# The third block's recurrent branch: order of its column chunks and gate products, packing of the gates' weights, and a few operations on other engines

## The reference, cut to what matters

```python
proj = h @ w_in                                  # 1024 x 2048
u, gate = split(proj)                            # 1024 columns each
uc = conv_b + sum_j up[:, j:j + T] * conv_w[j]   # causal, width 4
ub = uc.reshape(B, T, 4, 256)                    # four groups
r = sigmoid(einsum('btgi,gij->btgj', ub, w_rg) + b_rg)
i = sigmoid(einsum('btgi,gij->btgj', ub, w_ig) + b_ig)
log_a = -8 * r * softplus(-lam)
a = exp(log_a)
mult = sqrt(-expm1(2 * log_a));  mult[t = 0] = 1
h_t = a_t * h_(t-1) + mult_t * i_t * uc_t        # over all 272 rows
y = (h * silu(gate)) @ w_out
```

## Time and profile before

| | us |
|---|---|
| median of three runs | 2482.13 |
| lowest and highest of them | 2480.46, 2484.95 |
| the profiled execution | 2470.93 |
| its span, first to last instruction | 2469.5 |
| recurrent mixer to the end of the span, from PE's first column instruction at 2341.9 | 127.6 |
| PE, DVE, ACT, POOL busy in that stretch | 92.2, 85.2, 60.5, 0.0 |

### The profile page before, as it was taken

How to read it: one execution, slowest core, us unless ns; L and a number is a source line. 1 busy time by engine, 2 the same in 40 slices (tenths; PEclk the granted TensorE clock), 3 DMA queues, 4 the chain that set the end, 5 groups by cost and what they waited for, 6 DMA issues and landing times.

```text
span 2469.5 us, 29520 instructions
## 1 busy us (share of the span) xinstructions
PE 2040.5 (83%) x12478; PEld 1372.8 (56%) x12478; DVE 988.3 (40%) x1689; ACT 731.2 (30%) x1160; POOL 22.5 (1%) x27
## 2 busy tenths in 40 slices
PE   5998867777787777776778799889889899889895
PEld 3555412333333333342334499769888898766694
DVE  2542412211222221223434344577654545553475
ACT  4322221110111110113111243544444544434444
POOL 0000000000000000000000000000000000000000
PEclk7988889899999999888889899999999999899797
DMA  8948799999999999999999855434245455420430
GB/s 351 359 152 311 266 406 413 409 409 411 413 412 409 409 409 410 404 403 411 398 408 410 325 181 180 160 97 142 94 145 164 143 187 169 134 98 19 135 111 17
DMA packets 228243, 672.09 MB, mean 272 GB/s; under 512 B 11520, under 2 KB 134528, under 8 KB 187792
## 3 DMA queue, kind: packets, MB, share of 16 engines
q1 hardware_dynamic: 228112, 670.21, 71.5%
HBM read 669.12 MB, written 1.05 MB: 271 GB/s over the span
## 4 chain that ended last, share of the span: by engine, by line
PE 54%; DMA 30%; DVE 11%; ACT 4%; issue 1%; SPq 0%; POOL 0%; DVEq 0%; ACTq 0%
DMA ring<-in_w 21%; PE pb L227 12%; PE pb L228 11%; PE pb L229 11%; DMA ring<-in_w_a 5%; PE pb L1635 3%; DVE WB L310 3%; DMA ring<-in_w_in 3%; PE pb L677 2%; PE pb L1658 2%; DMA ring<-in_w_mod 1%; ACT WB L304 1%; PE pb L1619 1%; PE pb L840 1%; PE pb L868 1%
## 5 line engine op out<-in xcount | busy, mean ns | idle before, releaser
L310 DVE TENSOR_TENSOR WB<-ring,WB 128x1024 fp32r<-128x1024 f32 (+3 forms) x370 | 425.3, 1191 | 495.2 <-ACT WB L304 494.9
L304 ACT ACTIVATE WB<-ring 128x1024 fp32r<-128x1024 f32 (+3 forms) x370 | 361.3, 1025 | 774.4 <-DMA ring<-in_w_a 466.2
L227 PE MATMUL pb<-HH,WB 128*128 128x256 f32 (+1 forms) x1680 | 496.9, 296 | 15.5 <-DVE HL L3133 4.7
L228 PE MATMUL pb<-HL,WB 128*128 128x256 f32 (+1 forms) x1680 | 486.3, 289 | 0.0
L229 PE MATMUL pb<-HH,WB 128*128 128x256 f32 (+1 forms) x1680 | 485.6, 289 | 0.0
L1635 PE MATMUL pb<-ring,big 128*32 128x512 f32 x2048 | 296.5, 671 | 151.5 <-DMA ring<-in_w 134.1
L227 PEld LDWEIGHTS pb<-HH,WB 128*128 128x128 f32 x1680 | 332.2, 198 | 41.4 <-issue 21.6
L228 PEld LDWEIGHTS pb<-HL,WB 128*128 128x128 f32 x1680 | 332.2, 198 | 2.5 <-issue 2.4
L229 PEld LDWEIGHTS pb<-HH,WB 128*128 128x128 f32 x1680 | 331.6, 197 | 0.0
L1635 PEld LDWEIGHTS pb<-ring,big 128*32 128x32 f32 x2048 | 46.8, 113 | 366.1 <-DMA ring<-in_w 279.6
L1658 PE MATMUL pb<-ring,big 128*32 128x512 f32 x1024 | 168.3, 644 | 61.9 <-DMA ring<-in_w 53.9
(11 more groups left out here) (416 smaller groups left out, 1989.3 us busy)
## 6 DMA issues: line engine op xcount, KB each, us to landing
ring<-in_w SPq DMA_DIRECT2D x384, 1024.0 KB, 14.5
ring<-in_w_a SPq DMA_DIRECT2D x66, 1024.0 KB, 12.1
ring<-in_w_in SPq DMA_DIRECT2D x38, 1024.0 KB, 6.8
ring<-in_w_b SPq DMA_DIRECT2D x33, 1024.0 KB, 5.1
ring<-in_w_ada SPq DMA_DIRECT2D x32, 1024.0 KB, 6.8
ring<-in_w_mod SPq DMA_DIRECT2D x24, 1024.0 KB, 8.8
ring<-in_w_out SPq DMA_DIRECT2D x8, 1024.0 KB, 5.3
ring<-in_b_w_in SPq DMA_DIRECT2D x8, 1024.0 KB, 6.6
```

What stands on the lines that cost most here:

```text
L227: pe.matmul(o, l[0], r[0], start=start, stop=False)
L228: pe.matmul(o, l[0], r[1], start=False, stop=False)
L304: act.activation(WB[:, c % 2, 0, x:y], flat[:, x:y], ACT.Copy).then_inc(*A(("high", c, z)))
L310: dve.tensor_tensor(WB[:, c % 2, 1, x:y], flat[:, x:y], WB[:, c % 2, 0, x:y].bitcast(F32), ALU.subtract).then_inc(*V(("low", c, z), *([("f ...
```

## The change

- The chunks are put in another order: u's four chunks (s_3+12 to 15), a chunk with both gates' weights for groups 0 and 1 (16), the gate branch's first (17), both gates' weights for groups 2 and 3 (18), the gate branch's other three (19 to 21). A gate chunk is loaded by two DMAs of 512 KB.
- PE's order follows: u's columns, gate products of groups 0 and 1, columns of the gate branch, groups 2 and 3, three more column chunks. u's blocks use banks 0 to 3, all gate products banks 4 to 7, so that group g waits for the sigmoids of g-1.
- u's halves no longer lie over the input. They take the columns 272 to 407 of `HH` and `HL`, each block of 272 as two pieces of 136.
- The copy out of PSUM into `pad3` goes from DVE to ACT, with four buffers in place of two.
- The high and low halves, sigmoids, tanh and logarithms are done group by group among the chunks. Three groups of silu come after the square roots.
- POOL makes i*u, and a squared in place of ACT's exp(2 log_a).
- DVE's states and gating are separate steps: states(0), gated(0), gated(1), split of chunk 22, states(1) before the first operand; then one states(g) after each of two splits.

```diff
-           + [x for p in range(4) for x in (cols256(I["b_w_in_3"][0], 256 * p), cols256(I["b_w_in_3"][0], D + 256 * p))]
-           + [(I[n][0].rearrange("g (a p) n -> p g a n", p=128), 2048, "p (g a n) -> p g a n", dict(g=4, a=2))
-              for n in ("b_w_rg_3", "b_w_ig_3")] + rows2(I["b_w_out_3"][0]))
+           + [cols256(I["b_w_in_3"][0], 256 * p) for p in range(4)]
+           + [lru_gates(0), cols256(I["b_w_in_3"][0], D), lru_gates(2)]
+           + [cols256(I["b_w_in_3"][0], D + 256 * p) for p in range(1, 4)] + rows2(I["b_w_out_3"][0]))
...
+    def u_half(t, o):
+        return t[:, 2 * (o % 4):2 * (o % 4) + 2, T3:T3 + T3 // 2]
+    def u_halves(t, g):
+        return t[:, 4 * (g % 2):4 * (g % 2) + 4, T3:T3 + T3 // 2]
...
+        def recurrence_gates(c, g):
+            hi, lo = chunk(c)
             pe.wait_ge(*at("u_halves", g))
             for f in range(2):
                 for q in range(2):
+                    if f == 0:
+                        pe.wait_ge(*at("low", c, q))
+                    if g:
+                        pe.wait_ge(*at("ri", g - 1, f, q))
                     for kk in range(2):
+                        e = mm3(pe, PB[4 + 2 * f + q][:, 0:T3].rearrange("p (s t) -> p s t", s=2),
+                                (hi[:, q, g % 2, kk, 128 * f:128 * f + 128], lo[:, q, g % 2, kk, 128 * f:128 * f + 128]),
+                                (u_half(HH, 2 * g + kk), u_half(HL, 2 * g + kk)), kk == 0, kk == 1)
...
+        for p in range(4):
+            columns(s_3 + 12 + p, 2 * (p % 2), ("u_in", p),
+                    [("u_out", p - 2, f) if p >= 2 else ("turned", "b3", 4 + 2 * p + f, 0) for f in range(2)])
+        for g in range(2):
+            recurrence_gates(s_3 + 16, g)
+        columns(s_3 + 17, 0, ("g_in", 0), [("u_out", 2, f) for f in range(2)])
+        for g in range(2, 4):
+            recurrence_gates(s_3 + 18, g)
+        columns(s_3 + 19, 2, ("g_in", 1), [("u_out", 3, f) for f in range(2)])
+        columns(s_3 + 20, 0, ("g_in", 2), [("g_out", 0, f) for f in range(2)])
+        columns(s_3 + 21, 4, ("g_in", 3), [("ri", 3, 0, f) for f in range(2)])
...  ACT
+        sp_.upto(s_3 + 13)
+        pads(0)
+        sp_.upto(s_3 + 14)
+        pads(1)
+        high(0)
+        sp_.upto(s_3 + 15)
+        pads(2)
+        high(1)
+        sp_.upto(s_3 + 16)
+        pads(3)
+        sp_.upto(s_3 + 17)
+        sigmoids(0)
+        high(2)
+        sigmoids(1)
+        tanh(0)
+        high(3)
+        sp_.upto(s_3 + 18)
+        tanh(1)
+        silu(0)
+        sp_.upto(s_3 + 19)
+        sigmoids(2)
+        sigmoids(3)
+        tanh(2)
+        sp_.upto(s_3 + 20)
+        tanh(3)
         act.wait_ge(*last("a"))
         for g, p in enumerate(PAIRS):
             act.activation(al[:, p, :], al[:, p, :], ACT.Exp).then_inc(*A(("a", g)))
-        sp_.upto(s_3 + 22)
+        sp_.upto(s_3 + 21)
         for g, p in enumerate(PAIRS):
             act.wait_ge(*at("expm1", g))
             act.activation(ml[:, p, :], uT[:, p, :], ACT.Sqrt, scale=-1.0).then_inc(*A(("mult", g)))
+        sp_.upto(s_3 + 22)
+        for p in range(1, 4):
+            silu(p)
...  DVE
+        sp_.upto(s_3 + 13)
+        conv(0)
+        sp_.upto(s_3 + 14)
+        conv(1)
+        low(0)
+        sp_.upto(s_3 + 15)
+        conv(2)
+        low(1)
+        sp_.upto(s_3 + 16)
+        conv(3)
+        sp_.upto(s_3 + 17)
+        logs(0)
+        low(2)
+        logs(1)
+        low(3)
+        sp_.upto(s_3 + 19)
+        logs(2)
+        logs(3)
+        sp_.upto(s_3 + 20)
+        for g in range(4):
+            expm1(g)
+        sp_.upto(s_3 + 21)
+        states(0)
+        gated(0)
+        gated(1)
         sp_.upto(s_3 + 22)
+        states(1)
         dve_operand(dve, "wob", 0, gT3[:, 0, :], T3)
         for n in range(8):
             if n < 7:
-                recur(n + 1)
+                if n:
+                    gated(n + 1)
                 dve_operand(dve, "wob", n + 1, gT3[:, n + 1, :], T3)
             if n % 2 == 0:
                 sp_.upto(s_3 + 23 + n // 2)
+                if n < 4:
+                    states(n // 2 + 2)
...  POOL
+        for g, p in enumerate(PAIRS):
+            pool.wait_ge(*at("ri", g, 1, 1))
+            pool.tensor_tensor(bl3[:, p, :], bl3[:, p, :], uT[:, p, :], ALU.mult).then_inc(*G(("iu", g)))
+        for g, p in enumerate(PAIRS):
+            pool.wait_ge(*at("a", g))
+            pool.wait_ge(*last("g"))
+            pool.tensor_tensor(uT[:, p, :], al[:, p, :], al[:, p, :], ALU.mult).then_inc(*G(("a_squared", g)))
```

More of the change, by code:

```diff
@@ L281, in _build @@
            + rows2(I["a_w_out_3"][0])
[L282 to L284 removed]
+           + [cols256(I["b_w_in_3"][0], 256 * p) for p in range(4)]
+           + [lru_gates(0), cols256(I["b_w_in_3"][0], D), lru_gates(2)]
+           + [cols256(I["b_w_in_3"][0], D + 256 * p) for p in range(1, 4)] + rows2(I["b_w_out_3"][0]))
     def load_chunk(sp, c):
         src, n, pat, dims = CH[c]
[L288 removed]
+        if not isinstance(src, tuple):
+            load(sp, ("s", c), src, n, pat, **dims)
+            return
+        i, before = R.place(("s", c), False, 2)
+        sp.wait_ge(*at("free", before))
+        for q in range(2):
+            sp.dma_start(slot(("s", c), n, pat, **dims)[:, q], src[q]).then_inc(R.sem[i], 16)
     def halves_at(n):
@@ L2659, in _build @@
     gT3 = take(8, T3)
-    pad3 = [take(T3 + 3) for _ in range(2)]
+    pad3 = [take(T3 + 3) for _ in range(4)]
     al = take(8, T3)
@@ L2839, in pe_third, with columns @@
         pe_turn(pe, "b3", TLX, reg_3("b_norm"), lambda i: xn_3[:, i, :])
[L2840 to L2860, removed]
+        def columns(c, b, name, waits):
+            hi, lo = chunk(c)
+            for f in range(2):
+                pe.wait_ge(*at(*waits[f]))
+                for kk in range(8):
+                    if f == 0 and kk % 4 == 0:
+                        pe.wait_ge(*at("low", c, kk // 4))
+                    if c == s_3 + 12 and f == 0:
+                        pe.wait_ge(*at("XT", "b3", kk))
+                    e = mm3(pe, PB[b + f][:, 0:T3], (hi[:, kk, 128 * f:128 * f + 128], lo[:, kk, 128 * f:128 * f + 128]), XT(kk, 0, T3),
+                            kk == 0, kk == 7)
+                e.then_inc(*P((*name, f), *([("used", c)] if f else [])))
+        def recurrence_gates(c, g):
+            hi, lo = chunk(c)
             pe.wait_ge(*at("u_halves", g))
@@ L3130, in dve_third, with conv @@
-        sp_.upto(s_3 + 21)
-        for g, p in enumerate(PAIRS):
+        for f in range(4):
+            dve.memset(pad3[f][:, 0:3], 0.0).then_inc(*V(*([("pads",)] if f == 3 else [])))
+        def conv(p):
+            for f in range(2):
+                o, P_ = 2 * p + f, pad3[2 * (p % 2) + f]
+                dve.wait_ge(*at("u_out", p, f))
+                dve.tensor_scalar(uT[:, o, :], P_[:, 0:T3], col("conv_w_3", o), col("conv_b_3", o), ALU.mult, ALU.add).then_inc(*V())
+                for j in range(1, 4):
+                    dve.wait_ge(*last("v"))
+                    dve.scalar_tensor_tensor(uT[:, o, :], P_[:, j:j + T3], col("conv_w_3", 8 * j + o), uT[:, o, :],
+                                             ALU.mult, ALU.add).then_inc(*V(*([("u", p, f)] if j == 3 else [])))
@@ L3155, in dve_third, with states @@
-        recur(0)
+        def states(g):
+            o = 2 * g
+            dve.wait_ge(*at("mult", g))
+            dve.wait_ge(*at("iu", g))
+            dve.memset(ml[:, o:o + 2, 0:1], 1.0).then_inc(*V())
+            dve.wait_ge(*last("v"))
+            dve.tensor_tensor(bl3[:, o:o + 2, :], bl3[:, o:o + 2, :], ml[:, o:o + 2, :], ALU.mult).then_inc(*V())
+            dve.wait_ge(*last("v"))
+            for x in (o, o + 1):
+                dve.tensor_tensor_scan(ml[:, x, :], al[:, x, :], bl3[:, x, :], 0.0, ALU.mult, ALU.add).then_inc(*V(("state", x)))
```

106 lines of the change are left out of this document (40 added, 66 removed).

## The result

Four executions of each kernel: 2457.65 us median (2455.30 to 2462.37) against 2481.3 (2475.26 to 2484.95). The ratio is 0.9909, 95% interval 0.9885 to 0.9934: faster by 16 to 28 us.

A forecast was written before the change was run, and what follows sets the result against it. A bare chain of dependent ACT and DVE steps between gates and output product was the bound. 2408.25 + 37.65 + 1.0 = 2446.9 against 2459.9, 13.0 less, gave 2469.1 us; range 2462 to 2476.

The forecast's parts named there:

- the sum with exclusion: Last stage's timeline if POOL and DVE fully exclude each other, costing 4.5 us: T = 2408.25, rows end at 2446.9.
- T: End of the last expm1, where the part uncovered by PE work starts: 2403.75 without exclusion, 2408.25 with; wrong if beyond 2412.
- The last step of the sum: From profiled execution to median: execution 2457.9 against 2470.93, the difference taken off the median 2482.13, giving 2469.1.
- The clock: PE's clock after idles: 1.0 us put for the 3.4 idle before operand 0, nothing for the 2.35 before group 3.
- u's columns: PE's column chunks for u: DVE falls behind, chunk 15 starts 0.9 late, chunk 16 with the first gates 1.1 late.
- POOL beside DVE: i*u and squares on POOL meeting DVE instructions: 2.7 + 1.8 = 4.5 us by full exclusion, the upper end taken.
- Squares: a squared on POOL instead of ACT: 1.34 us each for 544 columns, a(0) to the last square 5.9.
- From the last expm1 on: DVE's last order and PE's output product: rows end 37.65 us after T plus 1.0 for the clock; PE idles 3.4.
- the signs of being wrong: Last stage: T beyond 2412, DVE's order from T idle over 2 us in sum, or gates above 0.2 each.
- Two-piece operand: Gates' moving tensor in two pieces of 136: cost 0, 2.9 kept for range; slower rival, 2498, chance 0.04.
- POOL undisturbed: Rival for i*u and squares: POOL and DVE don't disturb each other, gain 17.5, 2464.6 us; chance 0.24.
- Clock and crossings: Rival in the last stage: clock falls at both idles and engine crossings take longer, gain 9.2, 2472.9; chance 0.17.

The follow-up runs named there:

- e2: The changed kernel again, unedited, against the kernel before: stage 100.62 us, median 2458.5 us, ratio 0.9927.
- e6: The changed kernel with the copy from PSUM into the padded buffer back on DVE: stage 107.39 us, ratio 0.9969 against the kernel before.
- e9: The changed kernel with POOL's first i*u held until DVE has split chunk 18: stage 98.21 us, ratio 0.9907 against the kernel before.
- e8: The changed kernel with each square made twice on POOL: stage 105.71 us, ratio 0.9949 against the kernel before.
- e11: The changed kernel once more, unedited, against the kernel before: stage 100.59 us, median 2463.0 us, ratio 0.9929.
- e3: The changed kernel with i*u and the squares on DVE instead of POOL: stage 97.13 us, ratio 0.9900 against the kernel before.
- e4: The changed kernel with silu(0) after the roots and the last two column chunks in other banks: stage 97.90 us, ratio 0.9903 against the kernel before.
- e7: The changed kernel with close to the old order of DVE's last part: stage 103.40 us, ratio 0.9947 against the kernel before.

## Why the prediction was right or wrong

**The bound and the mechanism: right.** The chain between gates and output product was the stage's bound: PE's waits of 4.7 and 14.9 us there are 0.5 and 2.4 now. The change took 14.4 to 17.3 us out of the stage, 13.0 forecast. No run undoes the overlap alone; that it is the bulk of the gain is read from the two traces. In e2, group 3 began 47.2 us after the start (49.15 by the sum with exclusion, 2388.35 + 2.7 less 2341.9), the last expm1 ended at 63.0 (T, 66.35), and the rows ended 37.6 later (38.65): each part came a little earlier than put.

**The last step of the sum: wrong.** "That execution lies 11.2 below the median 2482.13; I take the difference off the median: 2469.1." The number it was taken from was no zero line. The start of the stage scatters by 17 us between executions of identical work, so a median of three executions is a draw: later medians of before on 11 to 28 executions were 2474.5 to 2479.24, each out of single times from 2468 to 2471 up to 2484 to 2487. Of the 11.45 between 2469.1 and 2457.65, 7.6 are the zero line (2482.13 against 2474.5), 3.0 the gain, put too small (13.0 against 16.0; 1.4 to 4.3 by the stages), and the last 0.8 the changed kernel's own four executions (2457.65 against 2458.5). Whether the zero line was high by chance or because those executions ran on another chip no run tells; in the stages and in the repeats nothing of it shows. The range carried the uncertain prices of the edits and nothing for this scatter of the measurement; the medians of before alone lie 7.6 apart, and 2462 less 7.6 would have held the result. The same scatter makes "A difference under 0.2% (5 us) can't be told from none here" a little too optimistic: the intervals here are 0.2 to 0.28% to either side with four to twelve executions.

**The clock: a draw.** Put at 1.0, with nothing for the 2.35 idle. The idle came as forecast (2.33 to 2.39), and the clock behind it fell in one profile of three. The two outcomes stand 3.0 apart, half of it behind this idle and half in the output product, so no single number was to be had.

**u's columns: size off by 0.9.** The first gate instruction came 27.7 after the start, forecast 28.6, since a convolution's four instructions take 1.95 from block to block and not 2.06. The idle before chunks 15 and 16 was 0.54 and 0.55, not 0.9 and 1.1. e6 shows how thin this is.

**POOL beside DVE: right in kind, about 0.7 too dear, and with a wrong reading.** Forecast 4.5; e9 gives 2.4 for i*u (2.7) and e8 1.4 for the squares (1.8). The rule of the Trainium skill that was weighed there ("SBUF — State Buffer", section Who interferes with whom) is borne out for two SBUF inputs: 3.52 and 2.44 in one meeting. DVE was held 1.17 and 1.10 by products of 1.36; a square that met expm1 was 0.48 longer, with 0.61 of expm1 still to run. "All read two tensors in SBUF" does not hold for the logarithm steps (L3194): they read one, and the first of them took 1.45 instead of 0.36 beside POOL's second product, so two tensors are no condition for being held. Nor does "The trace has no such meeting". In the kernel before, DVE's L593 reads two tensors in SBUF and begins while the last of POOL's L611 still runs:

```profile
1406.69 1.49 POOL L611 TENSOR_TENSOR HL<-tmpT,HH 128x256 fp32r<-128x256 f32 x2 [0.35 <-ACT HH L600]
...
1407.85 0.95 DVE L593 TENSOR_TENSOR HL<-tmpT,HH 128x256 fp32r<-128x256 f32 x2 [2.31 <-ACT HH L600]
```

In all three such pairs of L593 the first takes 0.61 and the second, with POOL done, 0.41. POOL, which had begun first, keeps its time; it was DVE's rows that had to be looked at. They would have spoken against "0" before any run, and so against the rival that got 0.24.

**Squares: too dear by 0.25 each.** The price 1.34 came from instructions with two different tensors; al*al took 1.09. That the same tensor twice is the reason is not shown: the squares also write to another tensor than they read, where i*u writes in place.

**From the last expm1 on: right.** 37.65 and 1.0 for the clock were forecast; 39.2 in the first profile, 37.6 in e2. PE idled 2.4 before operand 0 (3.4). One of the signs of being wrong did come true by its letter: DVE's order from T has 5.4 us of idle time in e2, over the 2 allowed. Most of it are waits for ACT's halves and splits that the sum had inside its terms of 2.7 and 3.0, so the sign was badly drawn; T itself (63.0 to 64.4 after the start, 70 allowed) and the gates (0.13 each, 0.2 allowed) stayed clear of theirs.

**Two-piece operand: no cost, as put.** Group 3 in e2 took 3.08 for 24 instructions, the contiguous columns 0.126 each. That rival, the only one on the slow side, falls.

**POOL undisturbed: false** (e9), though its gain of 17.5 is nearly what e2 and e11 gave (17.3): other terms were too dear by as much. **Clock and crossings, gain 9.2: false**; the clock did fall once, and the gain was still 14.4.

## What to carry to other kernels

Price a change in a stage whose length repeats better than the whole (here to 0.03 us before and, with PE's clock falling or not, to 3 us after), and give the absolute time with the scatter of everything ahead of it: a median of three is not a zero line. When work is moved to an idle engine, ask which instruction of the other engine it will meet and whether both read SBUF, and look in the trace at the one that begins second; e9 and e3 show that the same work at another moment, or on the busy engine in its gaps, was 2.4 and 3.5 us better. Two functions of different tables in turn on one queue cost their loads (2.57, here 2.7 of the stage in e4) where another engine waits behind them.

## What the runs showed of the hardware

- POOL's product of two tensors of 544 columns took 1.36 to 1.43 alone, 2.44 beside a pair of DVE splits, which grew from 2.35 to 3.52, and 1.93 beside the end of it and a DVE step with one tensor in SBUF, which grew from 0.36 to 1.45. A product of a tensor with itself took 1.09.
- Where one of the two had begun, it kept its time and the second waited: DVE's L593 0.61 instead of 0.41 behind a product of POOL, POOL's square 1.57 instead of 1.09 behind expm1.
- The mean granted clock over group 3, after one and the same idle of 2.33 to 2.39 us, was 1.00 in two executions of the changed kernel and 0.68 in a third; with the same idle it was 1.00 in e7 and e8 and 0.58 in e6. 24 instructions of group 3 took 3.1 and 4.5 to 4.6.
- A table load on ACT lasted 1.28, and the next activation began 1.29 after its start.
- Matrix instructions whose moving operand was in two pieces of 136 columns kept the pace of contiguous ones (0.128 and 0.126 from start to start).
